# A transformer block on split fp32 operands: high and low parts of an activation tile side by side, aligned buffers, token-major squares and output

## What is computed

```python
def pool_layer(x, mem, ...):
    proj = rmsnorm(x, norm_g) @ w_in                  # 2048 x 4096
    ... memory_attention(qm, mem, mem_g, w_mem_kv)    # rmsnorm(mem) @ w: 2048 x 1024
    return x + concat([y_pool, y_mem]) @ w_out        # 2048 x 2048
def nsa_layer(...):                                   # shared kv: 2048 x 3072
    proj = rmsnorm(x, norm_g) @ w_in                  # 2048 x 4132
    return x + concat([y_nsa, y_mem]) @ w_out
# second block: qkv 2048 x 6144, w_o 2048 x 2048,
# gate and up 2048 x 5632 each, down 5632 x 2048
out = x * rsqrt(mean(x*x) + eps) * final_g            # final norm, [256, 2048]
```

## Time and profile before

| | us |
|---|---|
| median of 3 runs | 2088.69 (2088.55 to 2091.04) |
| the profiled execution | 2088.68 |
| its span, first to last instruction | 2086.9 |
| busy: TensorE, VectorE, ScalarE, GpSimd | 2051.0, 1482.5, 1021.6, 483.1 |

### The profile page before, as it was taken

How to read it: one execution, slowest core, us unless ns; L and a number is a source line. 1 busy time by engine, 2 the same in 40 slices (tenths; PEclk the granted TensorE clock), 3 DMA queues, 4 the chain that set the end, 5 groups by cost and what they waited for, 6 DMA issues and landing times.

```text
span 2086.9 us, 29262 instructions
## 1 busy us (share of the span) xinstructions
PE 2051.0 (98%) x11470; PEld 1754.1 (84%) x11470; DVE 1482.5 (71%) x2056; ACT 1021.6 (49%) x1508; POOL 483.1 (23%) x442
## 2 busy tenths in 40 slices
PE   7999999999999999999999999999999999999997
PEld 6788888888788888888878888888888888888886
DVE  8866778789777556876656668777776557777765
ACT  5445444466533554654455555444444344454443
POOL 8305553300000344330212225211010000110122
PEclk9999999999999999999999999999999999999998
DMA  7555566566654333555444445555556665555664
GB/s 251 171 185 156 178 188 197 184 207 221 221 179 160 119 104 122 183 198 191 162 153 150 144 149 186 188 182 188 185 187 181 186 193 184 189 183 184 184 186 131
DMA packets 104089, 370.03 MB, mean 177 GB/s; under 512 B 11632, under 2 KB 12944, under 8 KB 103824
## 3 DMA queue, kind: packets, MB, share of 16 engines
q1 hardware_dynamic: 103952, 368.16, 55.2%
HBM read 366.02 MB, written 2.10 MB: 176 GB/s over the span
## 4 chain that ended last, share of the span: by engine, by line
PE 92%; DVE 6%; ACT 1%; issue 0%; POOL 0%; DMA 0%; DVEq 0%; ACTq 0%
PE psg L531 51%; PE psg L533 24%; DVE s_w L1622 2%; PE psg L578 2%; PE psg L580 2%; PE psg L579 2%; PE psg L530 2%; PE pst L531 1%; PE pst L617 1%; DVE s_rh L1640 1%; PE pst L533 1%; DVE s_ry L1640 1%; PE pss L793 1%; PE pso L813 0%; ACT s_w L1084 0%
## 5 line engine op out<-in xcount | busy, mean ns | idle before, releaser
L1622 DVE TENSOR_TENSOR s_w<-s_stage,s_w 128x1024 fp32r<-128x1024 f32 (+2 forms) x699 | 871.1, 1247 | 368.8 <-ACT s_w L1084 365.6
L1084 ACT ACTIVATE s_w<-s_stage 128x1024 fp32r<-128x1024 f32 (+2 forms) x699 | 728.3, 1043 | 789.2 <-PE psg L531 423.7
L531 PE MATMUL psg<-s_ry,s_w 128*128 128x512 f32 x2656 | 939.0, 401 | 3.7 <-DVE s_mv L1689 2.5
L533 PE MATMUL psg<-s_ry,s_w 128*128 128x256 f32 x2486 | 698.7, 281 | 0.0
L531 PEld LDWEIGHTS psg<-s_ry,s_w 128*128 128x128 f32 x2656 | 490.9, 189 | 116.3 <-issue 4.1
L533 PEld LDWEIGHTS psg<-s_ry,s_w 128*128 128x128 f32 x2486 | 470.8, 189 | 7.3
L531 PE MATMUL psg<-s_rh,s_w 128*128 128x512 f32 x1280 | 458.6, 404 | 11.9 <-DVE s_rh L1640 9.5
L533 PE MATMUL psg<-s_rh,s_w 128*128 128x256 f32 x1180 | 332.4, 282 | 0.0
L531 PEld LDWEIGHTS psg<-s_rh,s_w 128*128 128x128 f32 x1280 | 237.9, 189 | 65.2 <-issue 8.1
L531 PE MATMUL psg<-s_hid,s_w 128*128 128x512 f32 x704 | 245.9, 399 | 0.0
L533 PEld LDWEIGHTS psg<-s_rh,s_w 128*128 128x128 f32 x1180 | 224.6, 190 | 3.7
(11 more groups left out here) (388 smaller groups left out, 2224.8 us busy)
## 6 DMA issues: line engine op xcount, KB each, us to landing
s_stage<-in_wo SPq DMA_DIRECT2D x96, 512.0 KB, 3.5
s_stage<-in_wg SPq DMA_DIRECT2D x88, 512.0 KB, 3.5
s_stage<-in_wu SPq DMA_DIRECT2D x88, 512.0 KB, 3.6
s_stage<-in_ain SPq DMA_DIRECT2D x64, 512.0 KB, 3.6
s_stage<-in_wd SPq DMA_DIRECT2D x64, 448.0 KB, 3.4
s_stage<-in_wkv SPq DMA_DIRECT2D x32, 512.0 KB, 4.0
s_stage<-in_wd SPq DMA_DIRECT2D x32, 512.0 KB, 3.5
s_stage<-in_bq SPq DMA_DIRECT2D x24, 512.0 KB, 3.5
```

The source lines that it names most:

```text
L531: m = e.matmul(o, M.WH[:, r, ws], xx, start=begin, stop=end)
L533: m = e.matmul(o[:, T:2 * T], M.WL[:, r, ws], xh, start=False, stop=False)
L1084: e.activation(M.weights(c, 0, n), M.staged(c, n), ACT.Copy).then_inc(S["wh"], 1)
L1622: e.tensor_tensor(M.weights(c, 1, n), M.staged(c, n), M.weights(c, 0, n), ALU.subtract).then_inc(S["wl"], 1)
```

## The change

1. `RY`, `RH` and `HID` become `[128, 16 (22), 2, 256]`: high and low part of one tile are neighbours, and the 512 moving columns of line 531 are one run of 2 KB. All writers and readers change their index.
2. Small tensors are allocated first, then a filler up to a multiple of 1024 bytes, then the stage, the weights, x and the rest, so that these start at multiples of 1024.
3. The squares of the memory and of x are no longer made on GpSimd. Two token-major copies of the inputs (2 MB each, `memt` and `xt`) are loaded into a new tile `TM`; ScalarE squares them with a sum along the row (8 instructions of 512 columns each), VectorE adds the sums, the norm comes out as a column, and where it is needed as a row, VectorE scales the identity by it and TensorE spreads it with two matmuls of 128 columns.
4. The first weight unit is loaded in two halves by ScalarE's queue and split in halves (`first`); the gains of the memory come in a small load of their own, ahead of the memory, which now has six pieces.
5. The output is token-major: TensorE transposes the 16 tiles of x into eight PSUM banks, ScalarE and VectorE scale 512 columns at a time by the norm's column into `OT`, and eight stores of 128 x 512 follow.

```diff
-        self.RY = alloc(all_, "ry", [128, 2, KT, T], F32R)
-        self.RH = alloc(to2, "rh", [128, 2, KT, T], F32R)
+        self.RY = alloc(all_, "ry", [128, KT, 2, T], F32R)
+        self.RH = alloc(to2, "rh", [128, KT, 2, T], F32R)
...
+        self.PAD = fix("pad", [128, -((nc.sbuf_base + 31) // 32 * 32) % 1024 // 4])
+        self.ST = fix("stage", [128, NS, UW])
+        self.W = fix("w", [128, NR, 2, UW], F32R)
...
 def both(R):
-    return lambda k: (R[:, 0, k, :], R[:, :, k, :], R[:, 1, k, :])
+    return lambda k: (R[:, k, 0, :], R[:, k, :, :], R[:, k, 1, :])
...
-    w.wait_ge("sqx", KT)
-    norm_rows("x", [(ones, M.ACC[1][:, :])])
...
+    last = P.bank[("wd", 1), KT - 1]
+    vacant(("s", 0), ("s", 1), ("t", 0), ("t", 1), ("o", 0), ("o", 1), ("g", 1 - last[1]))
     w.wait_ge("sql", 15)
+    sums(M.ACC[1], True)
+    turn(0, 0)
+    turn(0, 1)
     w.wait_ge("sq15", 1)
+    sums(M.YT[0], False).then_inc(S["nr_mm"], 1)
+    for q in (1, 2):
+        turn(q, 0)
+        turn(q, 1)
+    w.wait_ge(*P.out[("wd", 1), KT - 1])
+    turn(3, 0)
+    w.wait_ge("nr_dve", 3 * NORM["fin"] + 1)
+    turn(3, 1)
...
+    def token_norm(n, rc, ticks):
+
+        i = NORM[n]
+        for _ in range(ticks):
+            yield
+        for t in range(2):
+            w.wait_ge(f"l_tm{i}", 16)
+            for q in range(4):
+                src = M.TM[:, t, 512 * q:512 * q + 512]
+                x = e.activation(src, src, ACT.Square, accum_out=M.CSQ[:, i, t, q:q + 1])
+            x.then_inc(S["sqt"], 1)
+            yield
...
+    for half, name in enumerate(("st_a", "st0")):
+        ws = slice(512 * half, 512 * half + 512)
+        e.dma_start(M.ST[:, 0, ws], P.units[0][0][:, ws]).then_inc(S[name], 16)
     tables()
...
     def token_norm(n, rc, ticks):
...
+        w.wait_ge("sqt", 2 * i + 2)
+        e.tensor_reduce(M.CSM[:, i, :], M.CSQ[:, i, :, :], AX.X, ALU.add).then_inc(S["csm"], 1)
+        yield
+        yield
+        refine(n, M.RC[rc][:, :], M.CSM[:, i, :], M.CW[:, 0:2], EPV[0] * D)
...
+        for t in range(2):
+            x = e.tensor_scalar(M.NW[:, t * 128:t * 128 + 128], M.con("ident", 128), M.RC[rc][:, t:t + 1], None, ALU.mult)
...
-    for j in range(KT):
-        w.wait_ge(f"l_x{j // 4}", 16)
-        square(M.ACC[1][:, :], j, M.X[:, j, :], "sqx")
...
+    e.dma_start(M.TM[:, :, :], A["memt"]).then_inc(S["l_tm0"], 16)
+    weight_units(2)
...
+        weight_units(2)
+    w.wait_ge("sqt", 2)
+    e.dma_start(M.TM[:, :, :], A["xt"]).then_inc(S["l_tm1"], 16)
...
+    for q in range(4):
+        for t, name in enumerate(("fin_act", "fin_dve")):
+            w.wait_ge(name, q + 1)
+            e.dma_start(out[t, :, 512 * q:512 * q + 512], M.OT[:, t, 512 * q:512 * q + 512]).then_inc(S["stored"], 16)
     w.wait_ge("stored", 128)
```

More of the change, by code:

```diff
@@ L619, in transposes, with token_rows @@
         held["t", 0] = held["t", 1] = ("at_pt", n + 1)
-    def mem_norm():
-        for _ in range(9):
+    def token_rows(n, ticks):
+        for _ in range(ticks):
             yield
-        w.wait_ge("sqm", KT)
-        norm_rows("mem", [(ones, M.ACC[0][:, :])])
-        yield
-        norm_cols("mem_c", [(ones, M.ACC[0][:, :])])
+        i = NORM[n]
+        vacant(("o", i % 2))
+        w.wait_ge("eps", 5)
+        w.wait_ge("nr_dg", i + 1)
+        for t in range(2):
+            m = e.matmul(M.PSO[i % 2][:, t * 128:t * 128 + 128], ones, M.NW[:, t * 128:t * 128 + 128], start=True, stop=True)
+        m.then_inc(S["nr_mm"], 1)
+        held["o", i % 2] = ("nr_rb", i + 1)
     def lam():
@@ L947, in tensor_program @@
     H0 = H
-    w.wait_ge("eps", 5)
-    side.start(mem_norm())
+    side.start(token_rows("mem_c", 15))
     group([("mk", 0, j) for j in range(4)], H, ready("m0"))
@@ L1064, in tensor_program, with turn, sums @@
         residual(("wd", hv), both(M.HID), ready("hid", 22 * hv), (0, 1, 2), 2, (8, 7, 7))
+    side.drain()
+    def turn(q, t):
+        for j in range(4 * q, 4 * q + 4):
+            w.wait_ge("xg", j + 1)
+            m = e.transpose(result(P, M, t, q)[:, 128 * (j % 4):128 * (j % 4) + 128], M.X[:, j, 128 * t:128 * t + 128], ident)
+        m.then_inc(S["turned"], 1)
+    def sums(acc, begin):
+        for t in range(2):
+            m = e.matmul(M.PSO[NORM["fin"] % 2][:, t:t + 1], acc[:, 128 * t:128 * t + 128], ones[:, 0:1], start=begin and t == 0, stop=not begin and t == 1)
+        return m
+    last = P.bank[("wd", 1), KT - 1]
+    vacant(("s", 0), ("s", 1), ("t", 0), ("t", 1), ("o", 0), ("o", 1), ("g", 1 - last[1]))
     w.wait_ge("sql", 15)
+    sums(M.ACC[1], True)
+    turn(0, 0)
+    turn(0, 1)
     w.wait_ge("sq15", 1)
-    norm_rows("fin", [(ones, M.ACC[1][:, :]), (ones, M.YT[0][:, :])])
-    side.drain()
+    sums(M.YT[0], False).then_inc(S["nr_mm"], 1)
[6 more added lines that the diff above has]
+    turn(3, 1)
 def scalar_program(e, S, P, M):
@@ L1135, in silu, with first @@
         e.activation(M.ET[i % 2][:, :], M.ZT[i % 2][:, :], ACT.Tanh).then_inc(S["z_t"], 1)
+    def first(half):
+        done[0], ws = 1, slice(512 * half, 512 * half + 512)
+        w.wait_ge(("st_a", "st0")[half], 16)
+        e.activation(M.WH[:, 0, ws], M.ST[:, 0, ws], ACT.Copy).then_inc(S[("wh_a", "wh")[half]], 1)
     def mem_rest():
@@ L1457, in residual @@
             post(j)
+    for half, name in enumerate(("st_a", "st0")):
+        ws = slice(512 * half, 512 * half + 512)
+        e.dma_start(M.ST[:, 0, ws], P.units[0][0][:, ws]).then_inc(S[name], 16)
     tables()
+    w.wait_ge("l_vec0", 16)
+    for j in range(8):
+        w.wait_ge(mem_piece(j), 16)
+        high(M.RH, j, M.MEM[:, j, :], M.vec("mg0", j), "m0")
+        if j in (0, 2):
+            first(j // 2)
+    split()
     split()
     w.wait_ge("l_vec", 16)
-    for j in range(8):
-        w.wait_ge(("l_mem0", "l_mem1", "l_mem2", "l_mem2")[j // 2], 16)
-        high(M.RH, j, M.MEM[:, j, :], M.vec("mg0", j), "m0")
-        if j in (3, 7):
-            split()
     side.start(mem_rest())
     side.start(mem1())
-    side.start(mem_norm())
+    side.start(token_norm("mem_c", 0, 9))
     nxt(8)
@@ L1474, in scalar_program @@
     side.start(setup())
+    side.start(token_norm("x_c", 1, 7))
     nxt(8)
     v_pair(("mv", 1), M.MV1[:, 1, :], 0, "mem_c")
-    norm_rows("x", 1, 0)
     nxt(8)
@@ L2132, in vector_program @@
     side.start(setup())
+    side.start(token_norm("x_c", 1, 9))
     nxt(4)
```

200 lines of the change are left out of this document (108 added, 92 removed).

## The result

The changed kernel takes 2074.56 us (median of 4 runs, 2073.35 to 2075.03) against 2088.62 us for the kernel before beside it: a ratio of 0.9929, 95% interval 0.9912 to 0.9947. The forecast was 2028.2 us, its range 1975 to 2064. The rival "layout is free" had given 2074.2. The profiled execution has a span of 2073.2 us, 13.7 us less than before.

A forecast was written before the change was run, and what follows sets the result against it. Bound by the rate at which wide matmuls follow each other on TensorE, plus a head paced by VectorE and a tail. 2088.7 less 46 + 12 + 2.5 = 60.5 gives 2028.2 us, range 1975 to 2064.

The forecast's parts named there:

- layout is free: Rival: the 10 ns come from something else in the units, only head and tail gains remain, 2074.2 us; chance 0.15.
- One run of 2 KB: Line 531's 512s (and line 750's) lose the second run's 10.0 ns each: 48.2 us over 4816, taken as 46.
- Alignment: Wide matmuls' buffers at multiples of 1024 bytes: 0 taken, 158 us upper bound together with the single run.
- excess of the pair over 322 ns: Pair of 512 and 256 at 353.2 ns against 322 from low-clock cycles: 31 ns, 149 us over 4800 pairs.
- The head: Start up to second key group: without GpSimd's squares VectorE speeds up, TensorE becomes the bound; 12 us less, bounds 2 and 17.
- the step's lower bound of 2 us: Least gain expected at the kernel's start, if only the earlier first matmul counts: 2 us.
- The loads: Two token-major 2 MB loads on the SP queue early on: nothing charged beyond 1.5 us of waits; rival's chance 0.05.
- The tail: After the last wide matmul: transposes take 7.6 us, the end comes 3.2 us earlier; 2.5 taken for low-clock risk.
- The middle: Some 100 early pairs gain less (1 us); around 400 to 570 us a faster TensorE waits more for weights (1 us).

The follow-up runs named there:

- blocks of sixteen: Changed kernel with wide-first order, but tile-closing units do their 256s first, so 512s and 256s stand in blocks of 16: 2055.95 us, ratio 0.9833.

## Why the prediction was wrong, step by step

*One run of 2 KB (46 us): wrong, and this is the step that failed.* It took the distance of 10.0 ns between the earlier trace rows for the price of the second run. The rows were read rightly but for rounding: over the whole stretch it is 236.2 ns, in the changed kernel and in the one before, and 226.7 ns in both for the other kind. But the two kinds of unit differ in three things, and the text named two, the runs and the roles. The third is that in one of them every other matmul is a 256. The rival "layout is free" had "the 256 beside it" in a clause, and said against it that nothing else in the rows set the two apart; the rows did, by the 256 that stands between any two 512s of the earlier trace rows and between none of the earlier trace rows. The old trace even holds a test of it, where a token-major unit follows a feature-major one:

```profile
92.60 0.28 PE L530 MATMUL pst<-s_ry,s_w 128*128 128x256 f32 x1
92.72 0.40 PE L531 MATMUL pst<-s_ry,s_w 128*128 128x512 f32 x1
92.95 0.40 PE L578 MATMUL psg<-s_w,s_ry 128*128 128x512 f32 x1
93.19 0.39 PE L579 MATMUL psg<-s_w,s_ry 128*128 128x512 f32 x1
93.41 0.39 PE L580 MATMUL psg<-s_w,s_ry 128*128 128x512 f32 x1
```

The first token-major 512 has one run and the weights as the moving side, and it still takes 233 ns, only two places behind a 256; the next takes 227. In the four such places of the trace it is 231 to 235 ns. A difference between two kinds of unit is a sum of all that differs and not the price of one of them. What the runs showed in place of the second run's 10 ns: with one run or two, aligned or not, a 512 in turn with a 256 takes 236.2 ns; with two runs and no 256 between, it takes 226.7. Of the 60.5 us, 46 stood on it; without it the sum gives 2074.2, and 2074.56 was measured. That they are so close is in part luck: of the 14.5 us left, the head was 2 us too high and the tail 1.1 too low.

*Alignment (0 taken, 158 as the bound): right.* 2073.78 us without it. The excess of the pair over 322 ns, on which the bound stood, is real but does not move with the addresses: up to 13 ns of it go with half the weight columns, and 18 stay with 64 columns too. What they are is open.

*The head (12 us): right in cause, and 10.05 us at the end.* The first matmul was put at 6 us and came at 5.97. The second key group was put at 55.7 and came at 57.19, 11.6 us earlier than before and not 13 (0.6 of the difference had been hoped for from the one run, with the first step); by the 17th unit it was 13.1, since the low clock behind the group is gone as well. The low parts fell from 886 to 481 ns as said, but VectorE's work in the first 69 us only to 48.0 us, not to 40, since it also does the work of the units that now fall in that stretch (in the first 60 us, up to the end of the 17th unit, it is 40.3). Of the two parts of the head the earlier start brought next to nothing: the step's lower bound of 2 us for it alone was too high, it is 0.2. What it didn't hold are the 0.9 us around the norm of x, which come from the new way to that norm, and 1.9 us near 640 us, mostly clock.

The Trainium skill, page "SBUF — State Buffer" (section "SBUF: two separate sides"), says that GpSimd and VectorE share one pair of ports, that an operation of VectorE with two operands in SBUF takes it against one of GpSimd that reads SBUF, and that the other waits meanwhile. The rows agree: the low parts read two tiles in SBUF and take 830 to 886 ns with GpSimd at work and 480 ns without. By the page the pair is held for a whole instruction, so a wait could last as long as one of GpSimd's, which are 0.8 us as a median here; the rows show 0.35 to 0.4 us for a low part.

*The loads (nothing charged): right.* In the first 69 us the DMA share rose from 0.67 to 0.86, and the second key group still came 11.6 us earlier; the old kernel without GpSimd's squares, which has no such loads, was there only at 57.78 us.

*The tail (2.5 taken, 3.2 worked out): 3.6, near by luck, since the path was another.* The transposes are 32 records, not 64, so they took less than the 7.6 us: the last begins 4.8 us behind the last wide matmul, and the last scaling ends 6.3 us behind it, where the sum had 8.9. But the sum had no term for the stores' issue. It begins 4.3 us behind the last wide matmul (before it was 5.8) and takes 4.04 us for the eight, one behind the other (before 6.33), so it goes on until 8.4 us behind; the end is 3.2 us later, about the 3.1 of before. I had taken 0.7 us off for a low clock that didn't come while TensorE had work.

*The middle (-1 and -1):* has no answer, since there was no faster TensorE. The blocks of sixteen give a hint: between 400 and 570 us, where TensorE waits for weights, 1.1 us of gain arrive of the 1.4 that 4.9 ns for each of the 288 pairs would be.

## What to carry to other kernels

Before a difference between two kinds of unit is taken for the price of one property, list all in which they differ, the neighbour in the queue included, and test the cheapest of them. Put matmuls of equal width in long blocks where the accumulation allows it: here it cost an order of loops, and gave 18.6 us where a new memory layout gave nothing. In a head that VectorE paces, look at what GpSimd does at the same time before looking at loads and starts.

## What the runs showed of the hardware

- A moving operand of 512 columns of 4 bytes costs the same as one run of 2 KB, as two of 1 KB that lie 4 KB or 16 KB apart, and at either offset modulo 1024 that was tried (0 and 128 bytes; in the kernel before the activations are at 896).
- At 2.4 GHz and with a new load of 128 columns each: 512s among themselves 226.7 ns, 256s among themselves about 120, the two in turn 236 and 117. A 512 behind 256s takes 233, 236, 228, 233, 231 and then 227 ns. With the 256 in another bank of PSUM the 512 of the pair takes 230.8. The first 256 behind a block of 512s takes 113. Why the disturbance lasts for five matmuls, and what the bank has to do with it, is open: shown is only that it nearly vanishes with 64 weight columns (and 64 output rows).
- GpSimd's squares of two inputs in the first 70 us cost this kernel 10.8 us (old) and 12.8 us (new), single runs each. They do it by way of VectorE: TensorE's waits for it in the first 120 us are 7.3 us longer in the old kernel. Much of the rest shows as a low clock: in its first 75 us 6 us more lie at the low level than without the squares, some 3 us of loss as an estimate.
- The low clock near 640 us, behind the run of 15-column matmuls, lasted 3.4 us in the old kernel, 6.8 us in the changed one and 10.2 us with blocks of sixteen; the old kernel without its squares had 6.8 us too. The runs don't say why.
